# Rotary embedding in a hybrid decoder layer: the swapped halves copied by ScalarE out of PSUM instead of moved by transfers, the first angle table made ahead of the first weighted sums

## The chip, the cores and the metric

One NeuronCore of a Trainium2 chip. The metric is the device time of one execution in microseconds (us). Five engines run at once, each with its own queue in order: TensorE (PE, products into PSUM), VectorE (DVE), ScalarE (ACT), GpSimd (POOL) and SyncE (SP), which only issues transfers here. They meet through semaphores. An instruction that waits holds up all that stands behind it on its engine.

## The reference, cut to what matters

One decoder layer on x of 512 tokens x 1024, float32. The first half projects the normalised x with one matrix whose columns are split into nine parts, rotates six of them by the tokens' positions, and feeds two groups of heads: sparse attention (8 heads of 64, with an indexer qi, ki, wi that selects 128 keys for each query) and retention (4 heads of 128).

```python
def _rope(x, positions):
    half = x.shape[-1] // 2
    freqs = ROPE_THETA ** (-jnp.arange(half) / half)
    ang = positions[..., None] * freqs
    x1, x2 = x[..., :half], x[..., half:]
    return concat([x1 * cos - x2 * sin, x2 * cos + x1 * sin])

mod = silu(c) @ w_ada + b_ada                  # 6 vectors of 1024: shift, scale, gate, twice
h = rms_norm(x) * (1 + scale1) + shift1
q_a, k_a, v_a, q_i, k_i, w_i, q_r, k_r, v_r, g_r = split(h @ w_in)
q_a, k_a, q_i, k_i, q_r, k_r are rotated        # _rope, heads of 64 or of 128
att = sparse_attention(q_a, k_a, v_a, q_i, k_i, w_i)
ret = silu(g_r) * rms_norm(retention(q_r, k_r, v_r))
x = x + gate1 * rms_norm(concat([att, ret]) @ w_out)
...                                            # then a mixture of 32 experts, top 2
```

## The kernel before, in words

All engines go through one list of steps that a planner (`Plan`) writes; each engine picks its part of a step. The work on a projection is cut into **units** of one PSUM bank. For the six rotated parts (qi, kw, ka, qa, qr, kr; kw is the indexer's key with its eight head weights) a unit holds 128 output features on the partitions by 512 tokens (384 for qi), each unit 8 products over k. For va, vr, gr the tokens are on the partitions. The order is qi 0 to 3, kw, ka 0 to 3, qa 0 to 3, va 0 to 3, qr, kr, vr, gr. Units take banks 0 and 1 in turn, so a unit can only start when the unit before the last has been read out. A rotated unit counts as read out when the semaphore `rope_ab` has its number.

Beside the units run, by the same list: from ka 1 on two indexer products for each unit (L842), whose relu ScalarE does (L1264) and whose weighted sum over heads VectorE does (L1759); from va 0 on attention scores (L877), their maximum (L1772, VectorE), exponential (L1272, ScalarE), scaling (L1283), transposes (L885), and values (L897); on VectorE also the weighted sums of the adaLN matrix (L1454, a `sums` step) and rounds of the selection of keys (L1528, L1529, a `keys` step). Behind ka 3, va 3 and kr 3 a `MOD` step follows: TensorE broadcasts an adaLN sum (L835) into banks 4 and 5, the same that the indexer's and attention's scores use.

A rotation is done in three parts. Feature i is paired with feature i + half of its head, and these stand on other partitions.

- `rotate` on VectorE (L1505 to L1517) reads the unit twice from PSUM: once times cos into its destination (L1514; for kw twice, L1514 and L1516), once times the signed sin into a buffer `CROSS` (L1517), which signals `rope_ab`.
- `swap` (L1233 to L1243), in ScalarE's queue at the unit's `sums` step, moves `CROSS` to `SWAPPED` across partitions by transfers: four pieces of 32 partitions (heads of 64) or two of 64 (heads of 128). `CROSS` and `SWAPPED` have two buffers each.
- `rotate` on GpSimd (L1992 to L1999) adds `SWAPPED` to the destination and signals `roped`. The indexer products wait for kw's, the attention scores for the last of qa, the retention scores for the last of kr.

GpSimd's queue also issues the four loads of an adaLN bias row (L2003), one behind each `MOD` step.

The kernel's front: VectorE forms four weighted sums of 8 steps each over w_ada chunks as they land, with waits for each half chunk; ScalarE squares and scales x; TensorE turns x; VectorE and ScalarE write the eight blocks of hT (L1492, L1221). Then VectorE makes both angle tables, for heads of 64 and of 128, in `angles` (L1461 to L1474), and ScalarE takes their sine and cosine (L1225, L1227); they lie in the upper half of `xs`. Both are done before the first unit is rotated.

## Time and profile before

| | us |
|---|---|
| median of 3 runs | 700.03 (698.43 to 700.11) |
| the profiled execution, own time | 697.74 |
| its span in the trace | 695.9 |
| TensorE products, busy | 629.8 (91%) |
| VectorE busy | 370.4 (53%) |
| ScalarE busy | 167.3 (24%) |
| GpSimd busy | 71.9 (10%) |

All rows are of that one profiled execution; times in the trace count from its span's start. The span ends 1.8 us short of the execution's time. By stage: the front with x, the first adaLN sums and hT until 43 us; the projections with indexer and attention until about 317; retention, output projection and routing until about 467; then the experts. Records give an engine's busy time and, in brackets, the idle time before an instruction with what ended it. A TensorE product of 128x512 shows as two records of the instruction, so a unit of 8 products is x16.

### The profile page before, as it was taken

The page shows a single profiled execution, that of the slowest core. Times are in us where ns is not written, and L with a number is a line of the kernel's source. Part 1 is how long each engine was busy: PE and PEld are TensorE (multiplying, and loading weights), DVE is VectorE, ACT ScalarE, POOL GpSimd, SP SyncE. Part 2 cuts the span into 40 slices and gives each one's busy share as a digit, 9 for nine tenths or more (in the row PEclk, how much of TensorE's full clock was granted, in tenths as well). Part 3 has the DMA queues.
Part 4 walks back from the last instruction along what each step waited for, and adds up shares of the span by engine and source line. Part 5 has one row for each costly group of instructions (what it writes and reads, how often), then busy time and mean ns, then how long its engine had stood idle before and what let it go on. Part 6 is the DMA issues. An engine that isn't in the chain of part 4 may idle for free.

```text
span 695.9 us, 7082 instructions
## 1 busy us (share of the span) xinstructions
PE 629.8 (91%) x2400; PEld 295.4 (42%) x2400; DVE 370.4 (53%) x742; ACT 167.3 (24%) x342; POOL 71.9 (10%) x75
## 2 busy tenths in 40 slices
PE   0598999959999999999989999989999999988983
PEld 0374444424444444446554456433434453433331
DVE  4777254987888675325984335872332333232055
ACT  1340000122423333441012223111212222221022
POOL 1001021110011111000000000112111111110101
PEclk9999999979999999999999999999999999998997
DMA  9993948080341819053089317899999999999996
GB/s 313 394 317 96 316 118 271 23 265 0 107 151 36 267 32 310 9 192 89 1 333 379 133 60 307 299 395 408 419 421 419 419 419 420 420 418 413 408 406 139
DMA packets 56532, 179.94 MB, mean 259 GB/s; under 512 B 10800, under 2 KB 11312, under 8 KB 45616
## 3 DMA queue, kind: packets, MB, share of 16 engines
q1 hardware_dynamic: 45136, 160.26, 60.4%
q0 software_dynamic: 6160, 12.10, 5.4%
q10 hardware_dynamic: 5200, 7.12, 3.8%
q8 instruction: 20, 0.33, 0.2%
q14 instruction: 16, 0.13, 0.1%
HBM read 168.43 MB, written 15.21 MB: 264 GB/s over the span
## 4 chain that ended last, share of the span: by engine, by line
PE 72%; DMA 10%; DVE 8%; issue 4%; SPq 3%; ACT 2%; ACTq 1%; POOL 0%; POOLq 0%; DVEq 0%
PE psum L1052 14%; PE psum L772 14%; PE psum L775 11%; PE psum L1113 8%; PE psum L920 7%; DMA both_bufs<-pair_rows 3%; DMA ring<-in_w_ada 2%; PE psum L1025 2%; SPq L647 2%; PE psum L877 2%; DMA both_bufs<-both_bufs 2%; PE psum L897 2%; PE psum L885 1%; PE psum L851 1%; PE psum L905 1%
## 5 line engine op out<-in xcount | busy, mean ns | idle before, releaser
L772 PE MATMUL psum<-hT,ring 128*128 128x512 f32 (+1 forms) x320 | 136.6, 581 | 2.3 <-DVE both_bufs L1517 2.3
L1052 PE MATMUL psum<-ring,hT 128*64 128x512 f32 (+2 forms) x320 | 92.2, 594 | 1.9 <-DMA ring<-in_w_up_exp 1.6
L772 PEld LDWEIGHTS psum<-hT,ring 128*128 128x128 f32 x320 | 60.4, 193 | 71.9 <-issue 60.7
L775 PE MATMUL psum<-ring,hT 128*128 128x512 f32 x192 | 87.1, 607 | 0.0
L1874 DVE TENSOR_SCALAR work<-work 128x256 f32<-128x256 f32 x16 | 4.6, 290 | 101.8 <-PE psum L1062 76.0
L775 PEld LDWEIGHTS psum<-ring,hT 128*128 128x128 f32 x192 | 36.4, 194 | 45.8 <-issue 45.6
L1454 DVE SCALAR_TENSOR_TENSOR rows<-ring,sm,rows 128x512 f32<-128x512 f32 x64 | 49.1, 767 | 8.7 <-DMA rows<-in_b_ada 7.1
L1052 PEld LDWEIGHTS psum<-ring,hT 128*64 128x64 f32 (+2 forms) x320 | 31.7, 142 | 49.0 <-issue 46.3
L1342 ACT ACTIVATE work<-psum 128x256 f32<-128x256 f32 x17 | 6.5, 384 | 146.6 <-PE psum L1052 146.6
L1113 PE MATMUL psum<-ring,work 128*64 128x512 f32 (+1 forms) x160 | 40.1, 598 | 0.7 <-ACT work L1348 0.7
L1052 PE MATMUL psum<-both_bufs,hT 128*64 128x512 f32 x64 | 31.1, 643 | 3.5 <-issue 3.5
L2043 POOL DMA_INDIRECT pair_rows<-work,pid_t x16 | 16.0, 1001 | 152.9 <-DVE work L1886 152.9
L1052 PE MATMUL psum<-xs,hT 128*64 128x512 f32 x64 | 31.1, 643 | 0.0
L1999 POOL TENSOR_TENSOR work<-work,both_bufs 128x512 f32<-128x512 f32 (+1 forms) x13 | 16.3, 1252 | 135.0 <-DMA both_bufs<-both_bufs 135.0
L795 PE MATMUL psum<-cst,work 128*64 128x1 f32 x64 | 8.3, 259 | 23.8 <-DVE work L1454 23.8
L920 PE MATMUL psum<-ring,work 128*128 128x512 f32 x64 | 28.7, 593 | 0.9 <-ACT work L1296 0.9
L920 PE MATMUL psum<-ring,hT 128*128 128x512 f32 x64 | 28.7, 594 | 0.7 <-ACT hT L1215 0.7
L1886 DVE TENSOR_SCALAR work<-psum,sinT 128x512 f32<-128x512 f32 x17 | 12.8, 751 | 29.9 <-PE psum L1113 25.4
L1876 DVE RECIPROCAL work<-work 128x256 f32<-128x256 f32 x16 | 28.0, 1753 | 0.5
L1052 PE MATMUL psum<-rows,hT 128*64 128x512 f32 x64 | 28.2, 593 | 0.0
L1528 DVE MAX8 sm<-score 128x8 f32<-128x256 f32 (+2 forms) x48 | 26.7, 556 | 1.2
L1264 ACT ACTIVATE both_bufs<-psum 128x256 f32<-128x256 f32 (+2 forms) x24 | 10.5, 488 | 68.7 <-PE psum L842 68.7
(309 smaller groups left out, 867.0 us busy)
## 6 DMA issues: line engine op xcount, KB each, us to landing
ring<-in_w_down_exp SPq DMA_DIRECT2D x20, 1024.0 KB, 18.6
ring<-in_w_in SPq DMA_DIRECT2D x8, 2048.0 KB, 10.6
ring<-in_w_ada SPq DMA_DIRECT2D x8, 2048.0 KB, 15.6
ring<-in_w_gate_exp SPq DMA_DIRECT2D x14, 1024.0 KB, 21.7
ring<-in_w_up_exp SPq DMA_DIRECT2D x14, 1024.0 KB, 24.4
ring<-in_w_ada SPq DMA_DIRECT2D x7, 1024.0 KB, 14.2
ring<-in_w_gate_exp SPq DMA_DIRECT2D x12, 512.0 KB, 14.9
ring<-in_w_up_exp SPq DMA_DIRECT2D x12, 512.0 KB, 15.1
```

Of the source, the lines that this page charges most:

```text
L647: sp.dma_start(chunk(n)[:, lo:hi, :], w_ada[:, lo:hi, what * 512:(what + 1) * 512]).then_inc(signal, 16)
L772: mm = pe.matmul(o[:, at], w[:, k, b * P:(b + 1) * P], hT3[:, k, at], start=(k == 0), stop=(k == KD - 1))
L775: mm = pe.matmul(o[:, :], hT3[:, k, b * P:(b + 1) * P], w[:, k, :], start=(k == 0), stop=(k == KD - 1))
L877: pe.matmul(o[:, 0:n], qaT[lo:lo + DH, h // 2, b * P:(b + 1) * P], kaT[lo:lo + DH, h // 2, 0:n], start=True, stop=True).then_inc(sc_done, 1)
L920: mm = pe.matmul(o[:, :], mixed, w[:, k, :], start=(k == 0), stop=(k == KD - 1))
L1052: mm = pe.matmul(o[rows, :], XT[u % 2][:, k, rows], both(GU_SLOT[place])[:, k, :, :], start=(k == 0), stop=(k == KD - 1))
L1113: mm = pe.matmul(o[rows, :], HT[u % 2][:, i, rows], down_of(DOWN_SLOT[place])[:, i, n * 512:(n + 1) * 512], start=(i == 0), stop=(i == KF ...
L1454: ins = v.scalar_tensor_tensor(out=acc, in0=w[:, k, :], scalar=sc_[:, k:k + 1], in1=acc, op0=ALU.mult, op1=ALU.add)
L1528: link(v.max(top8, m))
L1876: v.reciprocal(e, e).then_inc(gu_step, 1)
L1999: g.tensor_tensor(dst, dst, SWAPPED[r % 2][:, at], ALU.add).then_inc(roped, 1)
L2043: g.indirect_dma_start(out=y_dram, out_offset=bass.IndirectOffsetOnAxis(ap=pid_t[:, u:u + 1], axis=0), in_=YO[u % 2], in_offset=None, boun ...
```

## The change

- `swap` no longer issues transfers. It stands in ScalarE's queue at the `unit` step, waits for the unit, and copies its pieces from the PSUM bank to `SWAPPED` on the other partitions (4 or 2 activations with Copy). For kw the head weights are copied first.
- VectorE's `rotate` waits for these copies (`swapped`) and only multiplies by cos; the multiplication by sin is gone from it, `CROSS` too.
- GpSimd's `rotate` multiplies `SWAPPED` by the signed sin in place, then adds it to the destination: two operations where there was one. The sign in the constants is turned, since it now goes by the destination.
- The first angle table (heads of 64) is made ahead of all weighted sums, on VectorE and ScalarE, and lies where `CROSS` was; the second in VectorE's `sums` step of kw and ScalarE's of ka 0.
- SyncE's load of `decay` waits for the last rotation to be complete (`roped`) instead of `rope_ab`.

```diff
@@ tiles
-        trig = xs[:, 2048:4096].rearrange("p (n f t) -> p n f t", n=2, f=2)
-        posi = ropebuf[:, 0:S].bitcast(I32)
-        posf, turns = xs[:, 0:S], xs[:, S:2 * S]
-        CROSS = [ropebuf[:, i * S:(i + 1) * S] for i in range(2)]
+        trig = [home.rearrange("p (f t) -> p f t", f=2) for home in (ropebuf[:, 0:2 * S], xs[:, 2048:2048 + 2 * S])]
         SWAPPED = [ropebuf[:, (2 + i) * S:(3 + i) * S] for i in range(2)]
+        posi = SWAPPED[0].bitcast(I32)
+        posf, turns = T2[:, 0:S], T2[:, S:2 * S]
@@ SyncE, behind the load of gr
-                    sp.wait_ge(rope_ab, len(plan.rope))
+                    sp.wait_ge(roped, len(plan.rope))
@@ ScalarE
+            def sines(n):
+                act.wait_ge(ang_ready, n + 1)
+                a.activation(trig[n][:, 1, :], trig[n][:, 1, :], ACT.Sin, bias=zero,
+                             scale=cst[:, C_TRIG + 2 * n + 1:C_TRIG + 2 * n + 2]).then_inc(trig_ready, 1)
+                a.activation(trig[n][:, 0, :], trig[n][:, 0, :], ACT.Sin).then_inc(trig_ready, 1)
+
             act.wait_ge(cst_in, 16)
+            sines(0)
...
-            for n in range(2):
-                act.wait_ge(ang_ready, n + 1)
-                a.activation(trig[:, n, 1, :], trig[:, n, 1, :], ACT.Sin, bias=zero,
-                             scale=cst[:, C_TRIG + 2 * n + 1:C_TRIG + 2 * n + 2]).then_inc(trig_ready, 1)
-                a.activation(trig[:, n, 0, :], trig[:, n, 0, :], ACT.Sin).then_inc(trig_ready, 1)
@@ ScalarE, swap
-                act.wait_ge(rope_ab, r + 1)
+                act.wait_ge(unit_done, plan.unit[s] + 1)
+                if kind == "kw":
+                    a.activation(head_wts, bank(s)[DH:KW, :], ACT.Copy).then_inc(kw_out, 1)
                 if r >= 2:
                     act.wait_ge(roped, r - 1)
                 rows = pieces(kind)
                 for n, here in enumerate(rows):
                     there = rows[(n ^ 1) % 2] if kind == "kw" else rows[n ^ 1]
-                    act.dma_start(SWAPPED[r % 2][here, at], CROSS[r % 2][there, at]).then_inc(swapped[r % 2], 16)
+                    ins = a.activation(SWAPPED[r % 2][here, at], bank(s)[there, at], ACT.Copy)
+                ins.then_inc(swapped, 1)
...
-                elif s[0] == "sums" and s[1] in TURNED:
-                    swap(("unit",) + s[1:])
+                elif s == ("sums", "ka", 0):
+                    sines(1)
@@ VectorE, rotate
-                dve.wait_ge(unit_done, plan.unit[s] + 1)
+                dve.wait_ge(swapped, r + 1)
                 dve.wait_ge(trig_ready, 2 * table + 2)
-                if r >= 2:
-                    dve.wait_ge(roped, r - 1)
-                if kind == "kw":
-                    dve.wait_ge(kw_out, 1)
...
                 o = bank(s)[rows, at]
-                v.tensor_tensor(dst[rows, at], o, trig[rows, table, 0, at], ALU.mult)
+                ins = v.tensor_tensor(dst[rows, at], o, trig[table][rows, 0, at], ALU.mult)
                 if kind == "kw":
-                    v.tensor_tensor(dst[DH:2 * DH, :], o, trig[rows, table, 0, :], ALU.mult)
-                v.tensor_tensor(CROSS[r % 2][rows, at], o, trig[rows, table, 1, at], ALU.mult).then_inc(rope_ab, 1)
+                    ins = v.tensor_tensor(dst[DH:2 * DH, :], o, trig[table][rows, 0, :], ALU.mult)
+                ins.then_inc(rope_ab, 1)
@@ VectorE, sums
-                    if kind != "kw" and b < NB - 1:
+                    if kind == "kw":
+                        dve.wait_ge(x_n, NB)
+                        angles(1)
+                    elif b < NB - 1:
                         ada(ADA_BESIDE[kind], b, NB - 1)
@@ GpSimd, rotate
-                pool.wait_ge(rope_ab, r + 1)
-                pool.wait_ge(swapped[r % 2], swaps_to(r))
-                g.tensor_tensor(dst, dst, SWAPPED[r % 2][:, at], ALU.add).then_inc(roped, 1)
+                other = SWAPPED[r % 2][:, at]
+                table = 1 if kind in ("qr", "kr") else 0
+                pool.wait_ge(trig_ready, 2 * table + 2)
+                pool.wait_ge(swapped, r + 1)
+                g.tensor_tensor(other, other, trig[table][:, 1, at], ALU.mult).then_inc(crossed, 1)
+                pool.wait_ge(crossed, r + 1)
+                pool.wait_ge(rope_ab, r + 1)
+                g.tensor_tensor(dst, dst, other, ALU.add).then_inc(roped, 1)
```

What stands in a row on the engines, at the places that the next sections come to. On VectorE at the very front, before, the small steps on c are followed at once by the first weighted sum (`work<-ring`):

```order
L1433 TENSOR_TENSOR sm<-sm 128x8
L1452 TENSOR_SCALAR work<-ring,sm 128x512
L1454 SCALAR_TENSOR_TENSOR work<-ring,sm,work 128x512 x7
L1452 TENSOR_SCALAR work<-ring,sm 128x512
L1454 SCALAR_TENSOR_TENSOR work<-ring,sm,work 128x512 x7
```

The same place now (`rows` holds the positions and a scratch row, `both_bufs` the table):

```order
L1433 TENSOR_TENSOR sm<-sm 128x8
L1474 CAST rows<-both_bufs 128x512
L1464 TENSOR_SCALAR both_bufs<-rows,cst 128x512
L1465 TENSOR_SCALAR rows<-both_bufs 128x512
L1466 TENSOR_SCALAR rows<-rows 128x512
L1468 SCALAR_TENSOR_TENSOR both_bufs<-rows,both_bufs 128x512 x3
L1469 TENSOR_SCALAR both_bufs<-both_bufs 128x512
L1470 SCALAR_TENSOR_TENSOR both_bufs<-both_bufs 128x512
L1471 TENSOR_SCALAR both_bufs<-both_bufs 128x512
L1452 TENSOR_SCALAR work<-ring,sm 128x512
```

The ten operations of the first table have moved in front of the first sum. On ScalarE from kw to ka 3, before (`both_bufs<-psum 8x512` are the head weights, `both_bufs<-psum 128x256` the indexer's relus, DMA rows the swaps):

```order
L1252 ACTIVATE both_bufs<-psum 8x512
L1243 DMA both_bufs<-both_bufs 32x512 x8
L1264 ACTIVATE both_bufs<-psum 128x256 x2
L1243 DMA both_bufs<-both_bufs 32x512 x4
L1264 ACTIVATE both_bufs<-psum 128x256 x2
L1243 DMA both_bufs<-both_bufs 32x512 x4
```

The same place now:

```order
L1237 ACTIVATE both_bufs<-psum 8x512
L1243 ACTIVATE both_bufs<-psum 32x512 x8
L1194 ACT_TABLE_LOAD
L1194 ACTIVATE xs<-xs,cst 128x512
L1196 ACTIVATE xs<-xs 128x512
L1243 ACTIVATE both_bufs<-psum 32x512 x4
L1264 ACTIVATE both_bufs<-psum 128x256 x2
L1243 ACTIVATE both_bufs<-psum 32x512 x4
L1264 ACTIVATE both_bufs<-psum 128x256 x2
```

A unit's swap was behind its relus and is now ahead of them, and the second table's sines stand behind the copies of ka 0. On GpSimd one addition for each unit of 128x512 has become two operations, the second waiting for VectorE:

```order
L2000 TENSOR_TENSOR both_bufs<-both_bufs 128x512 [waits swapped,trig_ready]
L2003 TENSOR_TENSOR work<-work,both_bufs 128x512 [waits rope_ab,crossed]
L2000 TENSOR_TENSOR both_bufs<-both_bufs 128x512 [waits swapped,trig_ready]
L2003 TENSOR_TENSOR work<-work,both_bufs 128x512 [waits rope_ab,crossed]
L2007 DMA rows<-in_b_ada 1x16x64 [waits accB_clear]
```

The bias load of the second `MOD` step stands behind the rotation of ka 3 in both, but that rotation no longer waits for transfers.

## Rows read from the trace of the kernel before

**Rows 1.** Waits of TensorE until 330 us: who waited for whom, total, times, longest

```profile
PE psum L877 <- POOL work L1999: 7.6, 1, 7.6
PE psum L772 <- DVE both_bufs L1517: 2.3, 1, 2.3
```

**Rows 2.** Stretches: busy TensorE (records), granted clock, DMA share, GB/s; L868's wait

```profile
55.80:60.00 4.20, 4.17 (x8) 0.61 0.92 283
154.50:159.00 4.50, 4.46 (x9) 0.50 0.01 2
362.30:370.00 7.70, 4.62 (x22) 1.00 0.92 347
...
364.63 2.58 PE L868 MATMUL psum<-cst,work 128*128 128x128 f32 x16 [2.31 <-DVE work L1824]
```

**Rows 3.** Stretch of one unit of qa on VectorE: busy, granted clock, DMA

```profile
135.46:144.14 8.68, 8.26 (x20) 1.00 0.61 160
```

**Rows 4.** Timeline of TensorE: start, duration, instruction; qi 0 and 1, qi 2 and 3

```profile
43.03 10.53 PE L772 MATMUL psum<-hT,ring 128*128 128x384 f32 x32
...
55.83 12.28 PE L772 MATMUL psum<-hT,ring 128*128 128x384 f32 x32 [2.27 <-DVE both_bufs L1517]
```

**Rows 5.** ScalarE's groups by form (busy, mean ns), and single lines (ns min/median/max)

```profile
L1264 ACT ACTIVATE both_bufs<-psum 128x512 f32<-128x512 f32 x8 | 4.3, 595 | 9.4 <-PE psum L842 9.4
L1264 ACT ACTIVATE both_bufs<-psum 128x256 f32<-128x256 f32 x8 | 2.6, 381 | 37.7 <-PE psum L842 37.7
...
L1252 ACT ACTIVATE both_bufs<-psum x1: 588/588/588, 75.0 to 75.0; 8x512 f32<-8x512 f32 x1
L1999 POOL TENSOR_TENSOR work<-work,both_bufs x13: 987/1262/1766, 61.7 to 153.1; 128x512 f32<-128x512 f32 x9, 128x384 f32<-128x384 f32 x4
L1454 DVE SCALAR_TENSOR_TENSOR rows<-ring,sm,rows x64: 739/752/1635, 55.7 to 349.1; 128x512 f32<-128x512 f32 x64
```

**Rows 6.** Timeline from the end of qa 3 to va 1

```profile
138.10 0.92 PE L842 MATMUL psum<-work 64*128 64x384 f32 x4
138.95 7.13 PE L775 MATMUL psum<-ring,hT 128*128 128x512 f32 x16
...
144.14 0.69 DVE L1514 TENSOR_TENSOR work<-psum,xs 128x512 f32<-128x512 f32 x1
...
146.01 0.92 PE L842 MATMUL psum<-work 64*128 64x384 f32 x4
...
154.54 0.89 PE L877 MATMUL psum<-work 64*128 64x128 f32 x4 [7.61 <-POOL work L1999]
155.36 9.01 PE L775 MATMUL psum<-ring,hT 128*128 128x512 f32 x16
```

**Rows 7.** Front: the positions' issue and us to landing, VectorE's sums, its table

```profile
1.18 0.44 ACTq L1189 DMA_DIRECT2D both_bufs<-in_positions  x1
...
both_bufs<-in_positions ACTq DMA_DIRECT2D x1, 256.0 KB, 6.8
...
9.78 0.49 DVE L1452 TENSOR_SCALAR work<-ring,sm 128x512 f32<-128x512 f32 x1 [4.60 <-DMA ring<-in_w_ada]
...
29.80 0.49 DVE L1452 TENSOR_SCALAR work<-ring,sm 128x512 f32<-128x512 f32 x1 [2.21 <-DMA ring<-in_w_ada]
...
33.21 0.18 DVE L1481 RECIPROCAL sm<-sm 128x4 f32<-128x4 f32 x1 [0.46 <-ACT sm L1203]
...
33.86 3.12 DVE L1454 SCALAR_TENSOR_TENSOR work<-ring,sm,work 128x512 f32<-128x512 f32 x4 [0.48 <-DMA ring<-in_w_ada]
...
44.01:49.70 5.69, 5.38 (x12) 1.00 0.98 361
```

**Rows 8.** Timeline of TensorE behind ka 3

```profile
104.57 0.70 PE L842 MATMUL psum<-work 64*128 64x256 f32 x4
...
105.83 1.95 PE L835 MATMUL psum<-rows,cst 128*128 128x512 f32 x4 [0.56 <-ACT both_bufs L1264]
```

**Rows 9.** Page: mean busy tenths of the 16 DMA engines in 40 slices

```profile
DMA  9993948080341819053089317899999999999996
```

40 lines of the change are left out of this document (18 added, 22 removed).

## The prediction

> **What bounds the kernel now.** I read the chain of work that ended last, then the waits of TensorE in the first 330 us, then the timeline around each of its waits. Two thirds of the chain are TensorE's own products, and from the first projection (43.03 us) until the attention blocks are done TensorE stands still for hardly more than two things. It waits 7.6 us at the first attention scores (L877) for GpSimd's last addition of the rotation, and 2.3 us at L772 for VectorE [rows 1]. Each wait costs twice, because TensorE's granted clock falls with it: 0.61 in the stretch after the first and 0.50 after the second, where about 1.0 is granted elsewhere, so for a while 1.2 GHz instead of 2.4 [rows 2]. ScalarE and GpSimd are far from full, so what counts is when they deliver. VectorE is the engine to watch: in one unit of "qa" it is busy for 8.26 of 8.68 us [rows 3].
>
> **What the change removes.**
>
> *The first wait.* Before, VectorE makes both angle tables behind the last block of hT, while TensorE does qi 0 and qi 1; only then is the bank of qi 0 read, so that qi 2 starts 2.27 us late at 55.83 [rows 4]. After, the first table is there, ScalarE copies qi 0 as soon as it is done (some 5.3 us after 43.03, half of 10.53), and VectorE multiplies. Four copies of 384 columns are at most 4 x 0.54 us (the pace of the 512-column evictions of L1264, 4.3 us for 8 [rows 5]), with 0.1 us before and 0.7 us of multiplication behind, 3.0 us, and the next unit takes 5.3 us. So the wait goes whole. The two units behind it took 12.28 us where the two ahead took 10.53 [rows 4]; these 1.75 us of lower clock go too. Sum: **-4.0 us**. Next late would be the weights of qi 2, which are the chunk already in use.
>
> *The second wait.* The last unit of qa ends at 138.10; VectorE gets to it only at 144.14, since its own period (8.68 us [rows 3]) is longer than TensorE's (7.91, from 138.10 to 146.01); then come the multiplication, the transfers across partitions, and 1.26 us on GpSimd; TensorE, ready at 146.93, starts at 154.54 [rows 5, 6]. It needs the rotated qa 8.8 us after the end of qa 3 (va 0 and two indexer products lie between). After, ScalarE is done 0.1 + 4 x 0.54 = 2.3 us after the unit, GpSimd's multiplication of the swapped half 1.3 us later, at 3.5; its addition waits for VectorE too. If VectorE came as late as before (6.0), the sum would be ready at 6.0 + 0.7 + 1.3 + 0.2 = 8.2 us, still inside 8.8. It should come earlier: it loses one multiplication per unit (0.7 us; 8.7 becomes 8.0, TensorE's own pace), waits for the copies at most where it is early, and the wait of the first qa sum for its bias is eased since the queue of GpSimd no longer stands behind a swap by transfer when it is to issue it. I expect it about 3 us after the unit. So all 7.61 us go, and with them the clock: va 1 took 9.01 us where va 0 took 7.13 [rows 6]. Sum: -7.61 - 1.88 = **-9.5 us**.
>
> **What the change adds.**
>
> *In front.* VectorE waits for the positions, which land 6.8 us after their issue at 1.18, so at 8.0; a table takes 5.69 us; its weighted sums start at 13.7 instead of 9.78, 3.9 us later. It has waits of 2.21, 0.46 and 0.48 us before the end of the last of these sums, 3.15 in all, which take up most of that [rows 7]. **+0.8 us** on the path, since TensorE's turning of hT hangs on the last sum. Bounds: 0 if the positions land 0.8 us earlier; 3.9 if the covers were no covers. ScalarE's two sines and a table load lie in its long wait for x and cost nothing. SyncE's queue is not moved: its chunk loads wait for the sums of the chunks ahead, up to 4 us longer, but none of these (qi, kw, the fourth adaLN chunk, ka) is used within 10 us of its landing.
>
> *The second table* (5.7 us [rows 7] less a cast) stands on VectorE between the rotations of kw and of ka 0. VectorE idles there while TensorE does ka 0, and ka 0's rotation now waits for four copies anyway. Its sines and their table load go behind the copies of ka 0 on ScalarE, which then has nothing to do until ka 1 ends, 7 us later. Nothing.
>
> *The wait for the copies.* It stands at the head of VectorE's queue in each of 21 units; behind it are the unit's indexer or attention step and its weighted sum. A PSUM bank now comes free 0.1 + 2.2 + 0.7 = 3.0 us after its unit, with 7.1 us of the next unit to cover it. In qr and kr the swap is two copies, 1.1 us, in front of the eviction of turned probabilities; but those TensorE must first turn, behind the products with the values, while the copies run: nothing.
>
> *One place is on the path.* At the end of ka 3 TensorE does two indexer products and then the adaLN broadcast (L835) into the same two banks, so it waits for ScalarE's relu. Before, the relu runs at once: the unit ends at 104.57 and the broadcast starts at 105.83, 1.26 us later, 0.56 of it waiting [rows 8]. After, four copies stand ahead of it: 0.1 + 2.16 + 0.38 (one relu of 256 columns [rows 5]) + 0.1 = 2.74 us. **+1.5 us**. The other two broadcasts have no turned copies of four pieces before them.
>
> *GpSimd* gets 21 more operations of 0.99 to 1.26 us [rows 5], two per unit of 7 us or more: nothing by themselves. What they do to VectorE is the one rule that speaks against this change. The rows show a weighted-sum step that takes 0.75 us as a rule and 1.64 at the longest; GpSimd's addition takes 1.77 at the longest where 1.26 is its median [rows 5]. The Trainium skill (SBUF — State Buffer, section "SBUF: two separate sides") says that VectorE with two SBUF inputs and GpSimd hold one port pair in turn for a whole instruction, the other standing still. By the row a GpSimd operation costs VectorE up to 0.9 us, by the page all of its own length; the lengthened step is nearer to the row. I put it at nothing on TensorE's path, for VectorE at 3 + 4 x 0.9 = 6.6 us after qa 3 would be ready at 6.6 + 0.7 + 1.3 + 0.2 = 8.8, just in time.
>
> What a copy costs whose output lies on other partitions than its input no row shows. The nearest is L1252, 8 partitions x 512 in 0.59 us, [rows 5], about what full width takes: I take 0.54 in a row. It can't be below nothing; above, the end is the transfer it replaces.
>
> **The sum.** -4.0 - 9.5 + 0.8 + 1.5 = **-11.2 us**. Behind the attention everything is bound by TensorE or by loads that start on the ends of units, so it moves as a whole. The profiled execution took 697.74 us by its own time (span 695.9): it would take 686.5. The runs' median is 700.03; the same difference gives **688.8 us**. The runs of before spread by 1.7 us, so its own range is 687.5 to 690.
>
> **The rivals.**
> 1. *The clock falls at ka 3.* TensorE's wait there grows from 0.56 to 2.0 us. A wait of 2.27 us was followed by a lower clock [rows 2, 4], one of 2.31 at L868 was not (1.00 over the stretch with and after it) [rows 2], so it is open. Price: 1.75 us, time **690.5**.
> 2. *VectorE held up by GpSimd.* If each of the multiplications stopped it for a whole 1.26 us, it would come to qa 3 5.0 us later, and the rotated qa 10.2 us after the unit: a wait of 1.4 us at L877, and with a lower clock behind it 1.9 more. The skill's page named above would have it so. Time **690.2 to 692.1**, with rival 1 up to 693.8.
> 3. *The costs are covered.* Positions land early and the relu's delay is smaller: 2.3 us less, **686.5**.
> 4. *The gain is given back in the expert stage.* The transfer engines are at 90% or more from the 27th slice of 40 to the last but one [rows 9]. If the weights' stream set the end and did not start earlier, the time would stay, **698 to 700**. Against it: the stream's starts hang on unit ends, which move with TensorE.
> 5. *Slower: copies across partitions are slow.* ScalarE then paces the units. If a copy took 2.0 us, qi's four units would take 8.0 us each instead of 5.3 (+10.8), the eight from ka 0 to qa 3 8.7 with their relus instead of 7.9 (+6.4), and the relu at ka 3 would come 4 x 1.46 = 5.8 us later still: 23.0 lost against 11.2 won, time **711.8**. It decides from about 1.7 us per copy: 4 x (6.8 - 5.3) + 4 x 1.16 = 10.6, about what is won. L1252's row speaks against it, none excludes it.
>
> **How the numbers follow.** Chances: forecast 0.47, rival 1 0.22, rival 2 0.13, rival 3 0.08, rival 4 0.05, rival 5 0.05. Faster by over 0.3% (2.1 us, about what a measurement of this kernel can tell from no change) are the first four, 0.90; within 0.3% rival 4, 0.05; slower rival 5, 0.05. The range takes in the forecast, rivals 1 and 3 and most of 2, with some for the runs' spread: 686.0 to 693.5; it leaves out the upper end of 2, 4 and 5.
>
> **What would show it.** In the profile after: no wait of TensorE at the start of qi 2 and a granted clock near 1.0 there; L877 begins at once after va 0's indexer products, some 9.5 us closer to qa 3's end; the last sum of the front ends about 0.8 us later; L835 behind ka 3 starts 2.7 us after the unit; the copies take 0.5 to 0.6 us each. Wrong would be a copy of over 1 us, a granted clock of 0.6 behind L835, or weighted-sum steps of VectorE well above 0.75 us as a rule.

## The result, and the profile after

The changed kernel takes **694.74 us** (median of 5 runs, 692.94 to 696.76), the kernel before beside it 700.11 us (698.43 to 701.01): a ratio of 0.9934, 95% interval 0.9908 to 0.996. It is faster, by 5.4 us where 11.2 were forecast; 688.8 us was predicted and the range ended at 693.5. The profiled execution of after has a span of 694.9 us against 695.9, a difference of only 1.0, so the difference of the two profiles isn't the difference of the medians, and I come back to that.

First the waits of TensorE until 330 us in the kernel after, the view of [rows 1]: who waited for whom, total, times, longest.

```profile
PE psum L831 <- DVE sm L1768: 3.2, 2, 2.4
PE psum L831 <- ACT both_bufs L1264: 2.3, 1, 2.3
PE psum L873 <- ACT both_bufs L1264: 0.9, 2, 0.6
```

Both waits of [rows 1] are gone. In their place stand two waits of the adaLN broadcast (L831, L835 before): 2.3 us for ScalarE behind ka 3, and 2.4 us for VectorE behind va 3, which no step of the prediction names. The texts call these two the second and the third broadcast, by their number in the code. Neither wait is new: before, the second was 0.56 us [rows 8] and the third 1.10, with the full clock behind it:

```profile
187.73 1.96 PE L835 MATMUL psum<-rows,cst 128*128 128x512 f32 x4 [1.10 <-DVE sm L1772]
```

Here is TensorE's timeline after, in four pieces: the front, the second broadcast, the first scores, the third broadcast.

```profile
31.21 2.08 PE L791 MATMUL psum<-cst,work 128*64 128x1 f32 x16 [3.83 <-DVE work L1454]
33.22 5.49 PE L799 MATMUL psum<-cst 128*128 128x512 f32 x6
38.51 1.84 PE L811 MATMUL psum<-cst,work 128*128 128x128 f32 x12
40.28 2.08 PE L791 MATMUL psum<-cst,work 128*64 128x1 f32 x16
42.29 4.19 PE L811 MATMUL psum<-cst,work 128*128 128x128 f32 x20
...
46.32 20.81 PE L768 MATMUL psum<-hT,ring 128*128 128x384 f32 x64
...
103.59 0.70 PE L838 MATMUL psum<-work 64*128 64x256 f32 x4
106.64 2.89 PE L831 MATMUL psum<-rows,cst 128*128 128x512 f32 x4 [2.35 <-ACT both_bufs L1264]
...
148.51 0.92 PE L838 MATMUL psum<-work 64*128 64x384 f32 x4
150.00 0.87 PE L873 MATMUL psum<-work 64*128 64x128 f32 x4 [0.57 <-ACT both_bufs L1264]
150.80 7.13 PE L771 MATMUL psum<-ring,hT 128*128 128x512 f32 x16
...
182.63 3.64 PE L831 MATMUL psum<-rows,cst 128*128 128x512 f32 x4 [2.44 <-DVE sm L1768]
```

The four units of qi now stand in one line of 20.81 us, where before they were 10.53 + 2.27 + 12.28 [rows 4]. The first scores start 0.57 us after TensorE is ready for them (7.61 before), and va 1 takes 7.13 us instead of 9.01 [rows 6]. Both broadcasts that waited took longer themselves: 2.89 and 3.64 us, where 1.95 is the length at full clock [rows 8]. The stretches of after show the clock behind each wait; columns: length, busy (records), granted clock, DMA share, GB/s.

```profile
46.40:58.00 11.60, 11.60 (x38) 1.00 0.53 195
106.60:109.50 2.90, 2.86 (x5) 0.66 0.99 321
150.00:158.00 8.00, 8.00 (x22) 1.00 0.54 201
182.60:186.20 3.60, 3.56 (x5) 0.53 1.04 383
424.00:428.00 4.00, 4.00 (x15) 0.50 1.01 424
```

The front of the kernel before reads in the same view (L803 are three warming products, L799 after: products that nothing reads, in six records):

```profile
27.64 2.08 PE L795 MATMUL psum<-cst,work 128*64 128x1 f32 x16 [3.83 <-DVE work L1454]
29.71 4.40 PE L803 MATMUL psum<-cst 128*128 128x512 f32 x6
...
37.03 2.08 PE L795 MATMUL psum<-cst,work 128*64 128x1 f32 x16 [0.24 <-DVE work L1454]
39.04 4.20 PE L815 MATMUL psum<-cst,work 128*128 128x128 f32 x20
```

**One table for all runs.** I cut each profile at marks on TensorE: A from the first projection to the end of the broadcast behind ka 3; B on to the first scores (L873; it holds the second wait); C on to the end of the broadcast behind va 3; D on to the 128x2 products of the ranks in the router stage (L979); E from the first product of the experts (L1048) to the span's end. Each number is a difference of two starts or ends of the timeline, in us; the kernels below "after" are the experiments. The starts of the third front sum's products and of the first projection are given as times. Lines of the kernel before are 4 or 5 higher, those of some experiments up to 10.

| kernel | third sum | first projection | A | B | C | D | E | span |
|---|---|---|---|---|---|---|---|---|
| before | 27.64 | 43.03 | 64.75 | 46.76 | 35.15 | 247.57 | 249.1 | 695.9 |
| after | 31.21 | 46.32 | 63.21 | 40.47 | 36.27 | 250.27 | 249.1 | 694.9 |
| a1_changed | 32.62 | 47.71 | 63.22 | 40.46 | 36.26 | 250.27 | 249.4 | 696.6 |
| e1a | 27.84 | 43.30 | 64.23 | 39.92 | 35.98 | 253.29 | 249.0 | 695.0 |
| e2a | 31.55 | 45.09 | 60.48 | 39.71 | 35.78 | 248.21 | 248.3 | 687.2 |
| e6a | 31.97 | 44.85 | 62.26 | 39.72 | 34.57 | 250.18 | 249.2 | 690.0 |
| e4 | 31.60 | 44.77 | 63.09 | 40.58 | 33.25 | 253.30 | 249.3 | 693.5 |
| e3 | 31.68 | 45.00 | 62.93 | 40.75 | 34.99 | 248.47 | 248.7 | 690.3 |
| e9b | 31.24 | 43.85 | 63.65 | 40.03 | 34.19 | 248.52 | 249.0 | 688.8 |
| e7 | 32.38 | 45.67 | 63.16 | 40.52 | 36.26 | 250.30 | 249.4 | 694.6 |
| e11 | 31.20 | 44.40 | 63.05 | 40.62 | 36.24 | 250.38 | 251.2 | 695.1 |
| e8 | 27.76 | 43.22 | 60.95 | 39.71 | 34.58 | 248.75 | 248.8 | 685.3 |
| e9 | 27.87 | 42.22 | 60.95 | 39.71 | 33.82 | 251.28 | 248.7 | 685.9 |
| e10 | 27.58 | 42.83 | 60.94 | 39.72 | 33.82 | 249.51 | 253.6 | 688.1 |
| e12 | 31.58 | 44.83 | 63.00 | 40.67 | 36.17 | 248.68 | 252.0 | 693.8 |

A span is its first projection + A + B + C + D + some 9.3 us between D and E (8.5 in e12, 7.7 in e10) + E.

### The profile page after: what moved, and what is told of

Its sections match the earlier page's. It is cut to its first block, busy times and chain, and to the rows that moved or that the text cites. A ratio compares the mean times of both kernels' runs of the same rounds, so it can differ in the third digit from the quotient of the medians.

```text
span 694.9 us, 7089 instructions
## 1 busy us (share of the span) xinstructions
PE 633.0 (91%) x2400; PEld 298.1 (43%) x2400; DVE 375.2 (54%) x721; ACT 207.0 (30%) x411; POOL 100.5 (14%) x96
## 4 chain that ended last, share of the span: by engine, by line
PE 69%; DVE 15%; DMA 4%; issue 4%; SPq 4%; ACT 2%; DVEq 0%; ACTq 0%; POOLq 0%
PE psum L768 16%; PE psum L1048 13%; PE psum L771 8%; PE psum L916 7%; PE psum L1109 7%; SPq L540 4%; DMA ring<-in_w_up_exp 2%; DVE work L1454 2%; DVE score L1525 2%; DVE sm L1524 2%; DVE score L1755 2%; PE psum L1021 2%; PE psum L831 2%; PE psum L901 2%; DVE rows L1454 2%
## 5 line engine op out<-in xcount | busy, mean ns | idle before, releaser
L1048 PE MATMUL psum<-ring,hT 128*64 128x512 f32 (+2 forms) x320 | 93.9, 618 | 4.0 <-DMA ring<-in_w_up_exp 3.7
L771 PE MATMUL psum<-ring,hT 128*128 128x512 f32 x192 | 85.2, 597 | 0.0
L1243 ACT ACTIVATE both_bufs<-psum 32x512 f32<-32x512 f32 (+2 forms) x68 | 38.4, 564 | 77.8 <-PE psum L768 77.2
L1454 DVE SCALAR_TENSOR_TENSOR rows<-ring,sm,rows 128x512 f32<-128x512 f32 x64 | 55.5, 866 | 1.7
L1048 PEld LDWEIGHTS psum<-ring,hT 128*64 128x64 f32 (+2 forms) x320 | 32.2, 145 | 52.3 <-issue 48.9
L1048 PE MATMUL psum<-both_bufs,hT 128*64 128x512 f32 x64 | 29.7, 619 | 3.4 <-issue 3.4
L2000 POOL TENSOR_TENSOR both_bufs<-both_bufs 128x512 f32<-128x512 f32 (+1 forms) x13 | 15.5, 1192 | 103.0 <-ACT both_bufs L1243 103.0
L1048 PE MATMUL psum<-xs,hT 128*64 128x512 f32 x64 | 29.7, 619 | 0.0
L916 PE MATMUL psum<-ring,work 128*128 128x512 f32 x64 | 28.7, 593 | 0.9 <-ACT work L1296 0.9
L916 PE MATMUL psum<-ring,hT 128*128 128x512 f32 x64 | 28.7, 594 | 0.7 <-ACT hT L1218 0.7
L1048 PE MATMUL psum<-rows,hT 128*64 128x512 f32 x64 | 28.2, 593 | 0.0
```

Source lines behind the costliest of these rows:

```text
L771: mm = pe.matmul(o[:, :], hT3[:, k, b * P:(b + 1) * P], w[:, k, :], start=(k == 0), stop=(k == KD - 1))
L916: mm = pe.matmul(o[:, :], mixed, w[:, k, :], start=(k == 0), stop=(k == KD - 1))
L1048: mm = pe.matmul(o[rows, :], XT[u % 2][:, k, rows], both(GU_SLOT[place])[:, k, :, :], start=(k == 0), stop=(k == KD - 1))
L1243: ins = a.activation(SWAPPED[r % 2][here, at], bank(s)[there, at], ACT.Copy)
L1454: ins = v.scalar_tensor_tensor(out=acc, in0=w[:, k, :], scalar=sc_[:, k:k + 1], in1=acc, op0=ALU.mult, op1=ALU.add)
L2000: g.tensor_tensor(other, other, trig[table][:, 1, at], ALU.mult).then_inc(crossed, 1)
```

## The experiments

The kernel before took 698.8 us as a median beside all of them (ratios are to it).

**The change again**, as the measure for the others on that chip.

> The changed kernel itself, beside its variants on one chip. Its profile showed hT's first projection at 46.5 us instead of 43.0, a wait of 2.35 us at the adaLN broadcast behind ka 3 and one of 2.44 us behind va 3, each with a granted clock of 0.5 to 0.7 after it. If these belong to the kernel, they are here again within 0.3 us, and the time is 693 to 697. If they were an accident of that execution, one or the other is missing and the time is nearer 689.

Measured: 694.22 us (693.08 to 698.5), ratio 0.9939 [0.9919, 0.996]. B, C, D and A agree with the first profile to 0.01 us; only the front is later, by 1.4 us from the first sum on, which starts when the positions have landed. So what is lost between the marks is no accident of one execution. But in both sets the profiled execution is the one with the longest time (696.76, and here 698.5), so a typical execution loses less somewhere.

**First table behind hT again.**

```diff
-            angles(0)            # ahead of the sums
...
                                 ALU.add).then_inc(x_evV, 1)
+            angles(0)            # behind the last block of hT
...
-            sines(0)
...
                     swap(s)
+                    if s == ("unit", "qi", 0):
+                        sines(0)
```

> Only the first angle table goes back behind the blocks of hT on VectorE; its sines go behind the copies of qi 0 on ScalarE; the second table and all copies stay. Theory A (the table in front costs through TensorE's order: the third sum comes 3.6 us later, and the three warming products, the turns and the fourth sum's products stand behind it): first projection back at 43.0 to 43.3 us, no wait at qi 2, since one table instead of two ends at about 49.8, some 3.3 us less in all than the changed kernel, 691 to 692. Theory B (the table has to be in front, or qi 2 waits): a wait of 1 us or more at qi 2 with a lower clock behind it, and no gain over the changed kernel.

Measured: first projection at 43.30 us, 3.0 earlier than after, and qi 2 waits 0.20 us: so the early table buys hardly anything that copies out of PSUM don't buy alone, and costs the front. The time hardly moved all the same: 695.53 us, 0.9942 [0.9913, 0.9972]. The table shows where in its one profile: A is 1.0 us longer (the broadcast behind ka 3 took 3.44 us), and D is 253.3, 3.0 longer than after. These 3.0 us lie behind the wait for VectorE at L864 (L868 before), which is 2.31 us here as in [rows 2]:

```profile
358.55 3.03 PE L864 MATMUL psum<-cst,work 128*128 128x128 f32 x16 [2.31 <-DVE work L1824]
...
362.27 9.58 PE L916 MATMUL psum<-ring,hT 128*128 128x512 f32 x16 [0.69 <-ACT hT L1217]
```

After the same wait the two rows take 2.58 and 7.13 us in after, at the full clock; here the granted clock is 0.66 from 358.5 to 368.5 us.

**ka 3's copies behind the two relus.**

```diff
                 elif s in plan.rope:
+                    if s == ("unit", "ka", NB - 1):
+                        late = [s, 2]
+                        continue
                     swap(s)
...
                     a.activation(RELU[i % 2][:, 0:n], ...).then_inc(relu_ready, 1)
+                    if late[1] > 0:
+                        late[1] -= 1
+                        if late[1] == 0:
+                            swap(late[0])
```

> Only ScalarE's order at ka 3 is changed: the two indexer relus go ahead of the four copies. Theory A (the broadcast waits for the relu behind the copies, and the lower clock behind it is that wait's doing): the wait falls from 2.35 to about 0.6 us, the broadcast takes 1.95 instead of 2.9 us and qa 0 7.0 instead of 7.8, 3.4 us less up to qa 0's end. Theory B (the clock falls for another reason): the wait falls by 1.8 us, the broadcast and qa 0 stay long, 1.8 us less. In both VectorE's later lateness may eat a part at va 3.

ScalarE and TensorE in this kernel, behind ka 3:

```profile
103.08 0.66 ACT L1268 ACTIVATE both_bufs<-psum 128x256 f32<-128x256 f32 x2 [5.25 <-PE psum L838]
103.77 2.38 ACT L1243 ACTIVATE both_bufs<-psum 32x512 f32<-32x512 f32 x4
...
103.61 1.96 PE L831 MATMUL psum<-rows,cst 128*128 128x512 f32 x4 [0.56 <-ACT both_bufs L1268]
```

The wait is 0.56 us again, the broadcast takes 1.96, and A and B are 2.7 and 0.8 us shorter than after, 3.5 together: that is the whole price of four copies ahead of two relus, 1.8 us of it waiting and the rest clock. Time 689.8 us (689.01 to 693.6, four executions), 0.9896 [0.9848, 0.9945]: of the single edits it moves the median most, 4.4 us below the changed kernel's 694.22. The profile is of the one at 689.01. D also was 2 us shorter in it, by a higher granted clock in the router stage, which the edit does not explain.

**TensorE kept busy ahead of both waiting broadcasts.**

```diff
+                if m in (2, 3):
+                    stream(ps[7], 2)     # two 128x512 products that nothing reads
                 pe.wait_ge(ada_done, 2 * m + 2)
```

> Two products without use (about 1.8 us of TensorE) are put ahead of the adaLN broadcasts behind ka 3 and va 3, where TensorE otherwise waits 2.35 and 2.44 us; no engine waits less for another. Theory A (the lower clock comes from standing still): the broadcasts take 1.95 us each instead of 2.9 and 3.6, qa 0 7.0 instead of 7.8; 3.3 us less by the time of qr 0. Theory B (it does not): the broadcasts stay long, nothing gained.

Measured: 693.08 us, 0.9927 [0.9905, 0.9948]. Both broadcasts take 1.95 us:

```profile
102.75 1.98 PE L903 MATMUL psum<-cst 128*128 128x512 f32 x4
105.16 1.95 PE L833 MATMUL psum<-rows,cst 128*128 128x512 f32 x4 [0.43 <-ACT both_bufs L1266]
...
176.96 1.98 PE L903 MATMUL psum<-cst 128*128 128x512 f32 x4
179.45 1.95 PE L833 MATMUL psum<-rows,cst 128*128 128x512 f32 x4 [0.51 <-DVE sm L1770]
```

The deliveries are as late as before, but the clock stays; A + B are 1.7 us shorter and C is too. So of the 3.5 us at ka 3 and the 3 us at va 3 about half each is clock that fell with TensorE's standing still.

**GpSimd's addition left out**, then its multiplication: what holds VectorE up?

```diff
-                g.tensor_tensor(dst, dst, other, ALU.add).then_inc(roped, 1)
+                pool.sem_inc(roped, 1)
```

> The changed kernel with GpSimd's addition left out in all 21 units (the rotated vectors lack the swapped half times the sine, so the output is not the reference's); GpSimd's multiplication and all else stays. Question: what lengthened VectorE's pair of indexer steps (L1755 x2) behind each qa unit from 1.26 us before to 2.15 to 2.47 us. Theory A (GpSimd's addition starts with the pair, at the end of VectorE's multiplication, and the two engines hold each other up): the pair takes 1.3 us again, VectorE's period in qa falls from 8.9 to 8.0 us, the wait of TensorE for VectorE at the third broadcast (L831 at va 3, 2.44 us) falls to about 1.1 us and takes 2 us instead of 3.6, some 3 us gained there. Theory B (the steps are longer because of what they read, or because of the copies of ScalarE): the pair stays at 2.1 us or more and the wait at 2.4.

VectorE in qa 3 (L1755 is the pair of indexer steps behind the multiplication L1510), first after, with GpSimd's addition L2003, then without the addition:

```profile
146.41 0.69 DVE L1510 TENSOR_TENSOR work<-psum,both_bufs 128x512 f32<-128x512 f32 x1
147.02 2.15 DVE L1755 SCALAR_TENSOR_TENSOR score<-both_bufs,sm,score 128x384 f32<-128x384 f32 x2
...
147.25 1.50 POOL L2003 TENSOR_TENSOR work<-work,both_bufs 128x512 f32<-128x512 f32 x1 [2.73 <-DVE work L1510]
```

```profile
142.42 0.69 DVE L1510 TENSOR_TENSOR work<-psum,both_bufs 128x512 f32<-128x512 f32 x1
143.03 1.26 DVE L1755 SCALAR_TENSOR_TENSOR score<-both_bufs,sm,score 128x384 f32<-128x384 f32 x2
...
179.74 1.95 PE L831 MATMUL psum<-rows,cst 128*128 128x512 f32 x4 [1.10 <-DVE sm L1768]
```

The pair falls from 2.15 to 1.26 us, the period of VectorE in qa from 8.96 (137.45 to 146.41) to 8.07 (134.35 to 142.42), the wait at va 3 from 2.44 to 1.10, and C from 36.27 to 33.25. All numbers of theory A came out. It is 0.89 us of VectorE for a GpSimd operation of 1.26. The Trainium skill (SBUF — State Buffer, section "SBUF: two separate sides") has one of the two engines locked out of a shared port pair while the other's instruction runs; the trace agrees: the first step of the pair keeps its 0.61 us and GpSimd, which started meanwhile, took 1.50 instead of 1.26; the second step then took 1.50. The median did not follow: 695.01 us, 0.9932 [0.9906, 0.9957], with D at 253.3 in the profile, behind the same wait at L864 as in e1a (2.31 us, then 9.58 us for L916).

```diff
-                pool.wait_ge(trig_ready, 2 * table + 2)
                 pool.wait_ge(swapped, r + 1)
-                g.tensor_tensor(other, other, trig[table][:, 1, at], ALU.mult).then_inc(crossed, 1)
-                pool.wait_ge(crossed, r + 1)
```

> The changed kernel with GpSimd's multiplication left out in all 21 units (the swapped half is added without its sine, so the output is not the reference's); the addition stays. Theory A (what coincides with VectorE's pair is the addition): the pair stays at 2.1 us or more; L1454's weighted-sum step, 0.87 us on average after, may come closer to the 0.77 of before where the multiplication had fallen on it; the wait at va 3 stays at 2.0 us or more. Rival (any operation of GpSimd more costs VectorE its time): half of the loss of each unit comes back, period 8.4 us, wait at va 3 about 1.7 us.

Measured: 692.13 us (three executions), 0.9904 [0.9872, 0.9936]. The pair stays at 2.15 us, as theory A had it; the wait at va 3 is 1.86, between its 2.0 or more and the rival's 1.7, and C 34.99. L1454's mean falls to 0.816 us (0.866 after, 0.767 before), 3.2 us over 64 steps. So the addition accounts for the pair, and both operations for part of the weighted sums.

**The addition moved beside the key search**, with all work done.

```diff
                 elif s[0] == "keys":
+                    if s[1] == "qa":
+                        dve.sem_inc(searching, 1)
                     select_keys(...)
...
                 pool.wait_ge(rope_ab, r + 1)
+                if kind == "qa":
+                    pool.wait_ge(searching, b + 1)
                 g.tensor_tensor(dst, dst, other, ALU.add).then_inc(roped, 1)
```

> The changed kernel; in the four qa units alone GpSimd's addition waits in addition until VectorE begins its search for keys, whose steps have one operand in memory. All work is done. Theory A: the pair L1755 takes 1.3 us in all qa units, the search's steps keep their lengths (0.43, 0.41 us), VectorE's period in qa is about 8.0, the wait at the third broadcast is 1.1 us or less with a granted clock near 1.0 behind it, and the first projection of qr starts about 3 us earlier than in the changed kernel. The first attention scores (L873) start at most 0.5 us later than otherwise. Time 1 to 3 us below the changed kernel, the router stage varying by 2.5. Theory B (the sum of GpSimd's work counts, wherever it lies): the search is lengthened instead, and nothing changes at va 3.

The same view of VectorE, and GpSimd:

```profile
142.21 1.26 DVE L1755 SCALAR_TENSOR_TENSOR score<-both_bufs,sm,score 128x384 f32<-128x384 f32 x2
143.62 0.43 DVE L1524 MAX8 sm<-score 128x8 f32<-128x256 f32 x1
...
144.16 0.41 DVE L1525 MATCH_REPLACE8 score<-sm,score 128x256 f32<-128x256 f32 x1
...
143.70 1.27 POOL L2007 TENSOR_TENSOR work<-work,both_bufs 128x512 f32<-128x512 f32 x1 [1.66 <-DVEq L1786]
...
178.82 2.90 PE L831 MATMUL psum<-rows,cst 128*128 128x512 f32 x4 [1.10 <-DVE sm L1768]
```

Beside the search the addition costs neither engine anything: 0.43, 0.41 and 1.27 us are their lengths alone. (In qa 2 it started half a microsecond early, beside the last weighted sum, and took 1.67.) The same operation is free or dear by what lies beside it. But the expectation's reason, one operand in memory, is too simple. VectorE's first step of the second table that reads `xs` alone, in after and beside GpSimd's addition of kw (78.58, 1.50 us), is just as dear:

```profile
78.99 1.37 DVE L1465 TENSOR_SCALAR rows<-xs 128x512 f32<-128x512 f32 x1
```

Without the addition (e4) it takes 0.43 us. The multiplications by cos, which read one operand from PSUM, keep their 0.69 us beside GpSimd's. A granted clock near 1.0 was expected behind the wait, and it was 0.65 (broadcast 2.90 us) where the same wait of 1.10 left it whole in the run without the addition. Time 694.63 us (690.66 to 699.1), 0.9943 [0.9914, 0.9971]: as the changed kernel, where 1 to 3 us less were expected; its profiled execution is its lowest, 690.66.

**The three warming products of the front left out** (L799 and its waits; the expectation counts their six records).

```diff
-            for b in range(1, NB):
-                pe.wait_ge(x_ss, b)
-                warm(1)
```

> The changed kernel without the six products (L799, 128x512, 5.49 us) that TensorE does behind the third weighted sum only to keep busy. Question: why the first projection started 3.45 us later than before, though VectorE ended its fourth sum no later. Theory A (TensorE's own row hangs on the third sum: its products, the six products, twelve turns and only then the fourth sum's products; the waits of VectorE that should cover the longer front lie behind the third sum): the third sum's products and the first projection stood 15.3 us apart both before (27.64 to 43.03) and after (31.21 to 46.48); without the six products the fourth sum becomes the last to be waited for, and the distance falls to 12 to 13 us at full clock, to 14 with a lower granted clock at the turns. Theory B (the fourth sum or the eviction of hT is late): the distance stays at 15.3. Time: 3 us below the changed kernel at most, and as much above if the clock stays low for long.

The distance is 13.29 us (32.38 to 45.67), as theory A had it. It is no proof, though: TensorE then waits 2.17 us for ScalarE's normalized x, and the table shows seven kernels with the same front as after (e2a, e6a, e4, e3, e9b, e11, e12) whose distance is 12.6 to 13.5 with the three products in place. In all seven the granted clock is 1.00 from 39 us to the first projection, where after has 0.66 from 42 to 47. The front of e9b:

```profile
31.24 2.08 PE L791 MATMUL psum<-cst,work 128*64 128x1 f32 x16 [3.83 <-DVE work L1454]
33.25 4.35 PE L799 MATMUL psum<-cst 128*128 128x512 f32 x6
...
38.88 2.08 PE L791 MATMUL psum<-cst,work 128*64 128x1 f32 x16
...
43.85 6.62 PE L768 MATMUL psum<-hT,ring 128*128 128x384 f32 x20
```

4.35 us for the three products against 5.49 in after, the same instructions: their records start 0.85 us or more apart throughout in after, and in e9b 0.43 apart (the step at full clock) for the last two. So TensorE came to its full clock at about 36.5 us in e9b and behind the products in after. The profile's own clock shows 1.00 in both, because its records of the clock begin only there. Time without them 695.32 us, 0.9938 [0.9918, 0.9958]: nothing gained.

**Copies that stay on their partitions.**

```diff
-                    there = rows[(n ^ 1) % 2] if kind == "kw" else rows[n ^ 1]
+                    there = rows[n % 2] if kind == "kw" else rows[n]
```

> The changed kernel with ScalarE's copies staying on the partitions of their input (so nothing is swapped, and the output is not the reference's); as many copies of the same sizes. If crossing partitions costs something, the copies are shorter than the 564 ns of the changed kernel, on average over all 68, and four at the end of ka 3 take less than 2.39 us; TensorE's wait at the second broadcast falls below 2.35. If crossing is free, as a 8x512 copy of 0.59 us in the kernel before suggests, all three numbers stay to 0.02.

All three numbers stay: the mean of the 68 copies is 563 ns (564 after), the wait behind ka 3 2.34 us. Crossing partitions costs ScalarE nothing; rival 5 is out. One execution, 696.97 us.

**The front, ka 3 and va 3 together**, then with the addition moved too. e8 is the edits of e1a and e2a, and two filling products ahead of the third broadcast alone; e9 adds the edit of e9b.

> The changed kernel with three edits at once: the first table behind hT as before (first sines behind the copies of qi 0), the copies of ka 3 behind the two relus, and two products that nothing reads in front of the third broadcast. If the losses found by the single edits add up: front -3.2 us, ka 3 -3.4, va 3 -1.7, so the first projection of qr starts at about 178 instead of 186.3 us. Of the time, 5 to 8 us below the changed kernel (686 to 689) if the router stage takes 69 to 72 us as in all profiles so far; if it takes 74 as behind the moved table alone, 690 to 691.

> The three edits of e8_front_relu_fill and GpSimd's addition of qa beside VectorE's key search. VectorE's pair behind the qa units 1.3 instead of 2.15 us, and the third broadcast no longer waits for VectorE (0.51 us behind two filling products with e8). The gain over e8 is 0 to 1.5 us in front of qr: 687 to 688.5 us, if the router stage is the same.

Measured: **688.49 us** (686.69 to 692.41), 0.9859 [0.9813, 0.9905], and **687.95 us** (686.33 to 690.55), 0.9849 [0.981, 0.9887]. qr starts at 178.5 and 176.7 us instead of 186.3, so the single losses do add up until there, and these two are the fastest kernels of the study, some 1.5% below the kernel before. Between the two there is no difference that the runs can tell; of the 1.7 us between their profiles at qr, 1.0 lies in the front, by clock.

**The router stage filled**, on top of e9 (e10) and alone (e12).

```diff
                 route(NB - 2)
+                pe.wait_ge(mix_n, NB - 1)
+                stream(ps[6], 2)
                 turn_x2(NB - 1)
+                stream(ps[6], 2)
```

> e9_front_relu_fill_search with four more filling products in the router stage, two in front of the last turning of x and two behind it, where the granted clock fell to 0.50 in some profiles and not in others. Theory A (the lower clock there comes from the thin products and the short wait): the stretch from the last turn to the end of the broadcast has a granted clock near 1.0 in all runs, the stage takes 69 to 70 us, and the median is at e9's fastest runs, 685 to 687 us. Theory B (it comes by itself, or from the transfers that start there, 1.0 of the transfer engines' time): clock 0.5 to 0.6 as before, and the four products cost 0.9 us: 688 to 689 us. The six products in front (L799) stay.

> The changed kernel with nothing but the four filling products in the router stage (two in front of the last turning of x, two behind it). In the profiles so far the stretch from the end of the third broadcast to the rank products is 249 to 254 us long, with the granted clock of the router stage between 0.5 and 1.0; from the first product of the expert stage to the end of the span it was 249 us in nearly all profiles, and 253.6 in e10, where these four products had filled the router stage. Theory A (TensorE's arrival sets the end; what e10 lost in the expert stage was chance): clock near 1.0 in the router stage, the first product of the expert stage about 2 us earlier, 249 us behind it, median 2 us below the changed kernel (692.3). Theory B (the stream of weights, which holds the transfer engines full from about 418 us on, sets the end as soon as TensorE comes earlier against it): the expert stage grows by what TensorE gains, with TensorE waiting for its weights at about 605 and 620 us, and the median is that of the changed kernel (694.5) or 1 us above.

Measured: 690.39 us, 0.9879 [0.9847, 0.9912], and 694.99 us (693.85 to 696.24), 0.9938 [0.9913, 0.9962]. The stretches of the router stage, first after, then e12 (columns as above):

```profile
420.00:424.00 4.00, 3.58 (x24) 0.69 1.02 424
```

```profile
420.00:424.00 4.00, 4.00 (x18) 1.00 1.01 422
424.00:428.00 4.00, 4.00 (x23) 1.00 1.01 401
```

The clock obeys there: 1.00 instead of 0.69 and 0.50, and with e12 the first product of the experts comes 2.4 us earlier behind C (257.1 us instead of 259.5, D and the gap behind it). But E grows from 249.1 to 252.0 us, and to 253.6 in e10. The experts' products in e12, in the row where theory B expected TensorE to be held up:

```profile
605.13 3.65 PE L1112 MATMUL psum<-ring,work 128*64 128x512 f32 x16
609.40 0.61 PE L1051 MATMUL psum<-ring,hT 128*64 128x512 f32 x1 [0.61 <-issue]
```

That wait, with 0.61 us and in e10 1.31, stands in neither before nor after; the transfer engines are at 1.02 of their time there in e10. The median too is what theory B had. That the weights' arrival is what it waits for is an inference, since the profile puts the wait down to "issue", and most of the growth lies elsewhere. In e12 the first products of L1112 start 22.7 us after the stage's start (441.81 to 464.50), in after 21.5 (445.80 to 467.25): 1.2 us are lost 140 us ahead of that wait. The same products in after (L1048), then in e12:

```profile
457.73 7.09 PE L1048 MATMUL psum<-ring,hT 128*64 128x512 f32 x32
```

```profile
454.58 8.67 PE L1051 MATMUL psum<-ring,hT 128*64 128x512 f32 x32
```

The granted clock is 0.57 from 454 to 458 us in e12 (and from 448 to 452 in e10), where after has 1.00. In after it falls before the experts instead, to 0.58 from 438 to 442, among filling products that both kernels have there (L901, ten records: 6.23 us in after, 4.54 in e12). So the added products moved a fall of the clock from a place where it costs little into the expert stage. At the other end, TensorE's last product stands 1.6 us further from the end of the span than in after (680.81 to 693.8 against 683.52 to 694.9), and by that product the stage is only 1.3 us behind. What lengthens the last stretch is open.

## Why the prediction was wrong, step by step

The profiles of before and after, term by term:

| term | predicted | measured | how |
|---|---|---|---|
| first wait and its clock | -4.0 | -4.3 | 25.08 to 20.81 us for qi |
| second wait and its clock | -9.5 | -8.9 | 7.61 to 0.57, and 9.01 to 7.13 |
| front | +0.8 | +3.3 | 43.03 to 46.32 |
| ka 3 | +1.5 | +3.5 | A without qi +2.7, B without the wait +0.8 |
| va 3 | 0 | +3.0 | C +1.1, without the 1.9 of va 1 |
| router stage | 0 | +2.7 | D |
| rest | 0 | -0.3 | gap behind D |
| sum | -11.2 | -1.0 | 695.9 to 694.9 |

**What was removed** was right in size, and the reading that each wait costs twice held for both. The first scores did start at once but for 0.57 us (ScalarE's relu). One step in it was wrong and did no harm: the rotated qa was expected about 3 us after qa 3. VectorE came to it at 146.41, 5.8 us after the unit (140.60), hardly earlier than the 6.0 of before, and GpSimd was done at 148.75, 8.15 us after it, where TensorE needs it at 8.8. The 0.7 us of margin are those of the prediction's fallback sum (8.2), not of its forecast. What failed are the costs, and each in its own way.

**In front** the step that failed is "waits of 2.21, 0.46 and 0.48 us before the end of the last of these sums, 3.15 in all, which take up most of that". They do for VectorE: its last sum ended at 37.13 us (34.05 + 3.08) against 36.98 before. But TensorE's own row hangs on the *third* sum, whose products came 3.57 us later, since those waits lie behind it: three warming products, twelve turns, and only then the products of the fourth sum, which had been ready for 3 us at 40.28. How much of the 3.57 us remains goes by the granted clock, and it fell in both profiles while TensorE turned hT: 0.81 from 36 to 42 us and 0.89 from 42 to 47 before, 0.66 from 42 to 47 in after. Between these two the term is 3.3. Where the clock stayed at 1.00, the first projection starts at 43.85 to 45.09 us with the early table (seven profiles) and at 42.22 without it (e9): 1.6 to 2.9 us. That e9b's 43.85 is 0.8 us behind the profile of before, as forecast, is luck: before had lost about that much clock itself.

**At ka 3** the term was mis-sized and rival 1 came true. The broadcast started 3.05 us after the unit where 2.74 was worked out, and its wait was 2.35 us instead of 2.0. Most of that is the copies: four took 2.39 us, not 2.16, because 0.60 us each is their pace in a row. One relu of 0.38 follows ahead of the broadcast, as the prediction had it. Against before this is +1.8 us. The clock fell with it, +1.7 as rival 1 had priced it (1.75), and the relus moved ahead gave 3.5 back.

**At va 3** a term is missing. The prediction had VectorE faster by one multiplication per qa unit, "8.7 becomes 8.0". It became 8.96: 0.61 less for the multiplication, 0.89 more for the pair. (The weighted sums grew by 0.1 each over the whole kernel, 49.1 to 55.5 us for 64, but not in this unit: 2.33 us for three, before and after.) Rival 2 names this mechanism, but for the new multiplication, which in qa 2 and 3 falls beside the search and costs nothing; what costs is the addition, which now starts with the pair. The kernel before already showed it once, in qa 3, and there the pair is 0.7 us longer than its 1.26:

```profile
145.34 1.99 DVE L1759 SCALAR_TENSOR_TENSOR score<-both_bufs,sm,score 128x384 f32<-128x384 f32 x2
...
145.00 1.26 POOL L1999 TENSOR_TENSOR work<-work,both_bufs 128x512 f32<-128x512 f32 x1 [11.59 <-DMA both_bufs<-both_bufs]
```

And the prediction's check was made only at the first scores, where the delay is harmless, and not at the next place where TensorE waits for VectorE, the third broadcast. There 1.3 us more of waiting (1.10 to 2.44) and 1.7 us of clock were lost. Without the addition both are gone.

**Behind the attention** the statement that "it moves as a whole" failed. D goes with the granted clock at two places, whatever the edit. In the last 20 us ahead of L979 (the router stage) it is 0.91 in before, e2a, e3, e9b and e8, and 0.74 in the eight others without added products there; that is worth 1.7 to 2.8 us. In the 10 us from L864 on it is 1.0 in most, 0.83 or 0.84 in e8, e9 and e10, and 0.66 in e1a and e4, which is worth 3.0. Together they give D of 247.6 to 248.8, 250.2 to 251.3, and 253.3 us. Before was in the first group, after in the second, which gives back 2.7 of the 3.4 us that TensorE was ahead at the start of the retention units. What sets the clock there from one profile to the next is open. Rival 4 did not come true: without filling in the router stage, E stayed within 0.8 us of before in all but e11, and TensorE's arrival 10.3 us earlier in e8 (436.5 against 446.8 us) reached the end whole (685.3 against 695.9).

**Why the medians differ by 5.4 us and these two profiles by 1.0.** The profiled execution of before (697.74) lies below all five of its set, and that of after (696.76) is the highest of its five. It also has the lowest mean granted clock of them, 0.973, where the others have 0.975 to 0.982. The time goes with that clock: over the 73 executions of the kernel before beside the experiments the correlation is -0.71, with 0.49 us less for each 0.001 more. The median clock is 0.973 for before and 0.978 for after and a1, so some 2.4 us of the gain in the medians would go with the clock. It also fits that e1a and e4, which take losses away and gain nothing in the median, have 0.972 and 0.974, below a1's 0.978, and e2a 0.983. At which places the unprofiled executions won or lost it is not shown.

## What to carry to other kernels

A delay laid on one engine is covered only up to the point where another engine's row hangs on it: follow the consumer's instructions from the first late delivery, not the producer's to its last. When work moves to an idle engine, look at which instruction of the busy engine will run beside it, and place it beside instructions that a run shows to be untouched; counting operands in memory was not enough here. And a removed wait of TensorE is worth twice itself only if the waits that the change adds are also counted twice; a filling product or two in front of a wait that can't be avoided bought the second half back at ka 3 and va 3, while in the router stage the clock fell later instead.

## What the runs showed of the hardware

- ScalarE's copy out of PSUM to other partitions costs 0.60 us for 32x512 in a row, the same as on its own partitions (563 and 564 ns in the mean of 68).
- GpSimd's 128x512 addition beside a pair of VectorE's steps with two operands in SBUF costs VectorE 0.89 us and itself 0.24 (e4 against after); beside the table's step with one operand in SBUF it costs VectorE 0.94 (1.37 against 0.43, L1465); beside the search's steps neither loses anything (e9b, qa 3).
- The granted clock fell behind waits of 2.27, 2.35 and 2.44 us, and behind one of 1.10 us in e9b and not in e4 or before. Behind one and the same wait of 2.31 us ahead of L864 (L868 before [rows 2]) it stayed whole in ten profiles and fell in five (e1a, e4, e8, e9, e10); and in the router stage, with waits of 0.4 to 0.9 us among thin products, it was 0.50 or 1.00 from one profile to the next. So a price of the clock is a chance, not a term. The Trainium skill (TensorE: Matmul & The Clock Gate, section "What's actually happening") says that the window over which the clock is set runs free of the kernel's start; that would fit, and no run here shows it.
- TensorE at full clock with two products ahead of a wait kept its clock at that wait in all seven places so filled (ka 3 and va 3 in e6a, va 3 in e8, e9 and e10, the router stage in e10 and e12). It is no guard for what follows: in after the clock fell to 0.58 among ten records of filling products (438 to 442 us), and in e10 and e12 in the expert stage, 13 to 14 us behind its start.
